# The mixers' gate and branch products with tokens as stationary columns, 512 weight columns moving, and a transpose of the gated sum on TensorE

## The chip, the cores and the metric

The kernel runs on one core of one Trainium2 chip. The metric is the device time of one execution in microseconds (us). TensorE (PE in the profile) multiplies, VectorE (DVE) and ScalarE (ACT) copy, split and combine, GpSimd (POOL) does a few small powers, SyncE (SP) starts the transfers from HBM. A matmul of TensorE holds a 128x128 stationary operand, loaded by a weight load (PEld), and streams a moving operand of up to 512 columns past it into one of eight PSUM banks.

## The reference

Float32 throughout, 256 tokens, width 1024. Two layers of a first block, each with a mixer between two feed-forward parts, then two more mixers with their feed-forwards. The change is in the mixers of the first block, of which there are two:

```python
h = rms_norm(x, mix_norm[l])
(c_q, c_kv, k_rope, g_q, g_k, g_v, g_b, g_a, g_z, m_qkv, gate_logits) = split_cols(h @ w_in[l], IN_SPLITS)
o_mla, o_gdn, o_moba = ...                                # three branches, 512 wide each
branches = jnp.stack([o_mla, o_gdn, o_moba], axis=2)
up = jnp.einsum('bsnw,nwd->bsnd', branches, w_branch[l])  # 3 x (512 -> 1024)
gates = jax.nn.sigmoid(gate_logits.reshape(b, s, N_BRANCH, D_MODEL))
x = x + jnp.sum(gates * up, axis=2) @ w_out[l]
```

## The kernel before

All weights stream from HBM in units of 128x1024 floats (512 KB). A unit goes through four hands. SP loads it into one of three `raw` slots (L501). ACT rounds it to a first part `w_hi` (`split` on ACT, L558). DVE subtracts that from `raw` and so makes the rest, `w_lo` (L1229). TensorE uses the two parts in three products, high by high, high by low and low by high, with the activations `a_hi` and `a_lo`. There are six slots for split units, and the splits run five units ahead (`AHEAD`): ACT's `split(u + AHEAD)` waits until unit u-1 has been used. Every engine runs its own list of instructions in a fixed order that is written out by hand, with semaphores between the lists.

In a mixer, 24 gate units and 12 branch units are spread among the other work as fillers: TensorE runs them while other engines do the steps of the recurrence (`cover`), of the two softmax attentions (`FILLS`, four rounds each: fill, scores of the next pair, turn of P, fill, product with V) and of the projections between them. Gate units 0 to 3 stand in `cover`, 4 to 8 between the steps after it, 9 to 17 in the first attention, 18 to 21 after it, and the second attention has 22, 23 and branch units 0 to 7. Branch units 8 to 11 follow, and then the eight units of `w_out`.

One gate unit (`gate_unit`, by `fm`) makes 128 gate features of 256 tokens. Its stationary operand is a 128x128 block of weights and its moving operand is 256 tokens: 8 blocks of the contraction by 3 products, 24 matmuls of 256 columns into half a bank. ACT makes the tanh of it (`gate_tile`, L685, 128x256) and counts `gate_evac`. Units alternate between banks 6 and 7, so each waits for the tanh of the one before the last. One branch unit (`branch_unit`) makes 256 features of one branch in the same way, 24 matmuls of 256 columns into a whole bank, and DVE's `merge` multiplies it by (1 + tanh) into `mB` (L1465, counts `merge_read`) and adds that to `msum` (L1469). `msum` has features on partitions and tokens along, as the product with `w_out` wants its stationary operand, so ACT and DVE split it into `a_hi` (L910) and `a_lo` (L1826) straight from SBUF.

The lines that the next sections use, beside those: L694 and L696 are the exponentials of `exp_scores`, with their sums (ACT); L1434 to L1442 are `score_max`, which ends in `nmax_ready` (DVE); L1450 to L1452 are `normalise`; L1456 is `o_low`; L897 copies the turned keys (ACT); L1811 ends the keys of the second attention (DVE); L2168 is the helper of all matmuls; L2679, L2619 and L2452 are transposes.

## Time and profile before

| | before |
|---|---|
| time, median of 3 runs | 1932.98 us (1932.57 to 1933.21) |
| the profiled execution | 1932.31 us |
| its span in the trace | 1930.5 us |
| TensorE busy | 1922.0 us, 13137 matmuls |
| DVE, ACT, POOL busy | 1470.1, 1088.4, 85.6 us |
| DMA queue 1, share of 16 engines | 52.0% |

The span is the time from the first to the last instruction of the program; about 1.8 us of the execution lie around it. Matmuls overlap in the records (the end of each is modelled), so what a matmul costs is read from the distance between two starts, not from its own length. "Idle before" in the groups is the time in which an engine stood before an instruction, with the engine and line that released it.

### The profile page before, as it was taken

What the parts mean: (1) busy time and instruction counts of PE and PEld (TensorE: products, weight loads), DVE (VectorE), ACT (ScalarE), POOL (GpSimd) and SP (SyncE); (2) the same over time, 40 slices, a digit from 0 to 9 for tenths busy, and PEclk for the clock granted to TensorE, in tenths of its full rate; (3) what the DMA queues carried; (4) which work ended last, traced back from release to release, by engine and by line L of the source; (5) the groups of instructions that cost most, each with busy time, mean ns of one, the idle gap of its engine ahead of it and who ended that gap; (6) DMA issues with size and microseconds to landing.
All of it is one profiled execution on the core that took longest, in us unless ns stands there. A gap on an engine that the chain in (4) does not pass through costs nothing.

```text
span 1930.5 us, 35082 instructions
## 1 busy us (share of the span) xinstructions
PE 1922.0 (100%) x13137; PEld 1729.2 (90%) x13137; DVE 1470.1 (76%) x2252; ACT 1088.4 (56%) x1702; POOL 85.6 (4%) x61
## 2 busy tenths in 40 slices
PE   9999999999999999999999999999999999999999
PEld 8888999999888888889899998889898889889998
DVE  6777887777777777778777777777577888887887
ACT  6555764664555555567546644555355656676554
POOL 0000012010000000000110102000000000110000
PEclk9999999999999999999999999999999999999999
DMA  6656552344555555555424455655655555544654
GB/s 232 199 188 201 165 175 89 121 153 155 163 194 187 194 175 193 187 186 183 135 98 145 142 159 174 196 189 190 205 176 170 196 189 175 164 141 155 194 186 142
DMA packets 95798, 331.03 MB, mean 171 GB/s; under 512 B 10960, under 2 KB 16720, under 8 KB 95568
## 3 DMA queue, kind: packets, MB, share of 16 engines
q1 hardware_dynamic: 93712, 325.91, 52.0%
q10 hardware_dynamic: 1984, 3.68, 0.5%
q8 instruction: 74, 1.21, 0.3%
q14 instruction: 28, 0.23, 0.0%
HBM read 327.91 MB, written 1.64 MB: 171 GB/s over the span
## 4 chain that ended last, share of the span: by engine, by line
PE 93%; issue 3%; DVE 2%; ACT 1%; DMA 1%; POOL 0%; POOLq 0%; DVEq 0%; SPq 0%; ACTq 0%
PE ps L2168 91%; DMA raw<-stream 1%; DVE w_lo L1229 1%; PE ps L2194 1%; PE ps L2452 1%; PE ps L2679 0%; ACT w_hi L558 0%; DVE a_both L1286 0%; POOL sc L1144 0%; PE ps L2619 0%; DVE tmp L1254 0%; DVE a_both L1344 0%; DVE arena L1339 0%; ACT arena L783 0%; DVE sc L2032 0%
## 5 line engine op out<-in xcount | busy, mean ns | idle before, releaser
L2168 PE MATMUL ps<-a_both,w_hi 128*128 128x256 f32 (+1 forms) x4864 | 994.4, 325 | 0.4
L1229 DVE TENSOR_TENSOR w_lo<-raw,w_hi 128x1024 fp32r<-128x1024 f32 x614 | 749.9, 1227 | 236.3 <-ACT w_hi L558 235.5
L2168 PEld LDWEIGHTS ps<-a_both,w_hi 128*128 128x128 f32 x4864 | 813.4, 190 | 78.3 <-issue 3.2
L558 ACT ACTIVATE w_hi<-raw 128x1024 fp32r<-128x1024 f32 x614 | 637.1, 1053 | 139.5 <-DMA raw<-stream 91.6
L2168 PE MATMUL ps<-a_both,w_lo 128*128 128x256 f32 x3344 | 660.5, 283 | 0.0
L2168 PEld LDWEIGHTS ps<-a_both,w_lo 128*128 128x128 f32 x3344 | 524.4, 191 | 8.9
L2168 PE MATMUL ps<-w_hi,a_both 128*128 128x512 f32 (+2 forms) x1616 | 506.0, 383 | 0.3
L2168 PEld LDWEIGHTS ps<-w_hi,a_both 128*128 128x128 f32 x1616 | 300.8, 188 | 56.8 <-DVE a_both L1344 0.8
L2168 PE MATMUL ps<-w_lo,a_both 128*128 128x512 f32 (+2 forms) x808 | 308.6, 382 | 0.0
L2168 PEld LDWEIGHTS ps<-w_lo,a_both 128*128 128x128 f32 x808 | 152.4, 189 | 24.1
L629 ACT ACTIVATE a_both<-arena 128x256 fp32r<-128x256 f32 x132 | 55.3, 419 | 144.2 <-DVE arena L1339 101.1
L1144 POOL TENSOR_TENSOR sc<-sc,nhalf 128x2 f32<-128x2 f32 (+5 forms) x25 | 58.7, 2349 | 1620.8 <-DVE sc L1268 1185.9
L618 ACT ACTIVATE arena<-arena 128x256 f32<-128x256 f32 x88 | 36.7, 417 | 159.6 <-DVE arena L1331 143.9
L1298 DVE TENSOR_TENSOR arena<-ps,arena 128x512 f32<-128x512 f32 x114 | 78.6, 690 | 39.1 <-ACT arena L623 37.7
L623 ACT ACTIVATE arena<-ps 128x512 f32<-128x512 f32 x114 | 67.9, 596 | 65.9 <-PE ps L2168 65.8
L1331 DVE TENSOR_TENSOR arena<-arena 128x512 f32<-128x512 f32 x114 | 77.9, 684 | 0.0
L919 ACT ACTIVATE arena<-arena,par 128x256 f32<-128x256 f32 x44 | 26.5, 601 | 88.2 <-DVE arena L1331 78.4
L1344 DVE TENSOR_TENSOR a_both<-arena,a_both 128x256 fp32r<-128x256 f32 x132 | 56.4, 427 | 7.2 <-ACT a_both L629 7.2
L1837 DVE SCALAR_TENSOR_TENSOR arena<-arena,par 128x255 f32<-128x255 f32 x44 | 21.3, 484 | 37.6 <-ACT arena L919 37.5
L685 ACT ACTIVATE gates<-ps 128x256 f32<-128x256 f32 x48 | 18.5, 385 | 46.7 <-PE ps L2168 46.4
L2168 PE MATMUL ps<-arena 128*128 128x128 f32 (+4 forms) x400 | 43.8, 321 | 0.4 <-ACT gates L811 0.4
L1339 DVE SCALAR_TENSOR_TENSOR arena<-arena 128x256 f32<-128x256 f32 x88 | 39.0, 443 | 3.0
(334 smaller groups left out, 1238.5 us busy)
## 6 DMA issues: line engine op xcount, KB each, us to landing
raw<-stream SPq DMA_DIRECT2D x613, 512.0 KB, 3.4
arena<-upad SPq DMA_DIRECT2D x8, 284.0 KB, 5.4
gates<-late ACTq DMA_DIRECT2D x1, 1088.0 KB, 5.7
out<-tmp SPq DMA_DIRECT2D x8, 128.0 KB, 2.0
upad<-arena ACTq DMA_DIRECT2D x2, 288.0 KB, 7.7
con<-consts SPq DMA_DIRECT2D x1, 560.0 KB, 5.2
raw<-stream ACTq DMA_DIRECT2D x1, 512.0 KB, 4.3
x<-x_in SPq DMA_DIRECT2D x2, 256.0 KB, 5.4
```

Source lines behind the costliest of these rows:

```text
L558: nc.scalar.activation(w_hi[:, u % SLOTS, :], raw[:, u % RAW, :], ACT.Copy).then_inc(hi_ready, 1)
L618: nc.scalar.activation(th2[:, p, :], gus[:, p, 0:TOK], ACT.Tanh, scale=0.5).then_inc(gate_act, 1)
L623: nc.scalar.activation(glo, ps[:, 4 + 2 * p:6 + 2 * p, TOK:512], ACT.Copy).then_inc(lo_copied, 1)
L629: nc.scalar.activation(a_hi[:, 8 + p, :], gu2[:, p, :], ACT.Copy).then_inc(gu_hi_ready, 1)
L919: nc.scalar.activation(gh2[:, p, :], gus[:, p, 0:TOK], ACT.Identity, scale=w, bias=b).then_inc(conv_in, 1)
L1144: return nc.gpsimd.tensor_tensor(o, i, nhalf[:, 0:n], ALU.pow)
L1229: V.tensor_tensor(w_lo[:, u % SLOTS, :], raw[:, u % RAW, :], w_hi[:, u % SLOTS, :], ALU.subtract).then_inc(split_ready, 1)
L1298: V.tensor_tensor(gus[:, p, :].rearrange("p (a b) -> p a b", b=TOK), ps[:, 4 + 2 * p:6 + 2 * p, 0:TOK], glo, ALU.add).then_inc(gu_added, 1)
L1331: V.tensor_tensor(v, v, each(rrow, 2), ALU.mult).then_inc(gs_ready, 1)
L1339: V.scalar_tensor_tensor(gu2[:, p, :], a2[:, p, :], 0.25, gus[:, p, TOK:512], ALU.mult, ALU.mult).then_inc(gu_ready, 1)
L1344: V.tensor_tensor(a_lo[:, 8 + p, :], gu2[:, p, :], a_hi[:, 8 + p, :], ALU.subtract).then_inc(gu_split, 1)
L2168: return nc.tensor.matmul(o, a, b, start=start, stop=stop, **k)
```

## The change

Three things in the two mixers are written anew.

The operands of gates and branches change places. Each matmul now holds 128 tokens and streams 512 weight columns. The slots are loaded by another pattern (`RELAID`): a gate unit is two blocks of the contraction by 512 features, put together from four stretches of 256 columns (1 KB) per partition, and four such units make one group g of 512 features; a branch unit is two blocks by 512 features, from two stretches of 512 columns (2 KB), and two make a group. `token_half` is half a unit: 128 tokens, 6 matmuls of 512 columns into bank 6 (first 128 tokens) or bank 7 (the others). A unit is 12 matmuls. A group's sum stays in the two banks over all its units, so `gate_evac`, `merge_read` and the waits on them come once per group and token half, not once per unit.

ACT makes a tanh of 128x512 twice per group, for the first half at `gate_half` and for the second when the group's last unit is used; for three of four units `gate_tile` does nothing. DVE multiplies and adds in two parts of 128x512 for each branch group (`merge_factor`, `merge_add`). `msum` now has tokens on partitions, so TensorE turns it (`mix_turn`, 8 transposes for each half of the features) into banks 4 to 7, and the split for `w_out` reads those banks.

The order moves with it: two branch units (`branch_early`) go before the `up` units, gates 16 and 17 behind them, and the product order at the end is branch 8 to 10, the first half of 11, the first turn, the rest of 11, `w_out` 0 and 1, the second turn, `w_out` 2 to 7.

```diff
+        branch = group(("branch", l), 12)
+        take(("branch_early", l), branch[:2])
-        for n, name in ((1, "branch_gdn"), (2, "branch_moba"), (0, "branch_mla")):
-            take((name, l), [AT["branch", l] + 3 * dp + n for dp in range(4)])
+        take(("branch", l), branch[2:])
...
-EARLY_GATES = 18
+EARLY_GATES = 16
+BRANCH_OF = (1, 1, 2, 2, 0, 0)
+def gate_at(l, i):
+    return POS["gates", l] + i if i < EARLY_GATES else POS["late_gates", l] + i - EARLY_GATES
+def branch_at(l, i):
+    return POS["branch_early", l] + i if i < 2 else POS["branch", l] + i - 2
+def relaid():
+    at = {}
+    for l in range(DEPTH):
+        for i in range(24):
+            at[gate_at(l, i)] = (AT["gates_" + "abc"[i // 8], l] + i % 8 // 4 * 4, 1, 4, 256 * (i % 4))
+        for i in range(12):
+            g = i // 2
+            at[branch_at(l, i)] = (AT["branch", l] + 6 * (g % 2) + BRANCH_OF[g], 3, 2, 512 * (i % 2))
+    return at
+RELAID = relaid()
...
-         ((("g", 15),), (("g", 16),)))
-FILLS = (FILLS, (((("g", 22), ("g", 23)), (("b", 0),)),) + tuple(((("b", 2 * j - 1),), (("b", 2 * j),)) for j in range(1, 4)))
-LAST_FILL = (("g", 17), ("b", 7))
+         ((("g", 15),), (("b", 0),)))
+FILLS = (FILLS, (((("g", 20), ("g", 21)), (("g", 22),)),
+                 ((("g", 23),), (("b", 2),)),
+                 ((("b", 3),), (("b", 4),)),
+                 ((("b", 5),), (("b", 6),))))
+LAST_FILL = (("b", 1), ("b", 7))
...
+                elif u in RELAID:
+                    lo, step, n, col = RELAID[u]
+                    src = stream[lo:lo + step * n].rearrange("(i s) p n -> p i s n", s=step)
+                    sp.dma_start(raw[:, u % RAW, :].rearrange("p (i n) -> p i n", i=n), src[:, :, 0, col:col + UC // n]
+                                 ).then_inc(raw_loaded[u % RAW], 16)
...
+                if i % 4 < 3:
+                    return
+                act.wait_ge(gate_half, 6 * l + i // 4 + 1)
+                nc.scalar.activation(gate_part(i // 4, 0), bank(6), ACT.Tanh, scale=0.5).then_inc(gate_evac, 1)
-                nc.scalar.activation(gates[:, i, :], bank(6 + i % 2, 0, TOK), ACT.Tanh, scale=0.5).then_inc(gate_evac, 1)
+                nc.scalar.activation(gate_part(i // 4, 1), bank(7), ACT.Tanh, scale=0.5).then_inc(gate_evac, 1)
...
-                for dp in range(4):
-                    split(POS["branch_mla", l] + dp + AHEAD)
-                    if dp:
-                        mix_high(l, dp - 1)
+                for i in range(8, 12):
+                    split(branch_at(l, i) + AHEAD)
+                mix_high(l, 0)
+                mix_high(l, 1)
+                split(POS["out", l] + AHEAD)
+                split(POS["out", l] + 1 + AHEAD)
+                mix_high(l, 2)
-                for k in range(KC):
+                for k in range(2, KC):
-                act.wait_ge(mix_ready, 4 * l + dp + 1)
-                nc.scalar.activation(a_hi[:, 2 * dp:2 * dp + 2, :], msum[:, dp, :].rearrange("p (a b) -> p a b", b=TOK), ACT.Copy).then_inc(mix_hi, 1)
+                act.wait_ge(mix_turned, 4 * l + dp + 1)
+                nc.scalar.activation(a_hi[:, 2 * dp:2 * dp + 2, :], bank(4 + dp).rearrange("p (a b) -> p a b", b=TOK), ACT.Copy).then_inc(mix_hi, 1)
...
+            added_at = {}
+            def merge_factor(l, g):
+                n, h = BRANCH_OF[g], g % 2
+                if 2 < g < 5:
+                    need(added_at[g - 1])
+                elif g == 5:
+                    dve.wait_ge(mix_ready, 4 * l + 2)
+                for tt in range(TT):
+                    if tt == 0:
+                        dve.wait_ge(branch_half, 6 * l + g + 1)
+                        dve.wait_ge(unit_used, branch_at(l, 2 * g + 1) + 1)
+                    V.scalar_tensor_tensor(mB[:, tt, :] if g > 1 else msum[:, 2 * h + tt, :], gate_part(2 * n + h, tt), 1.0, bank(6 + tt),
+                                           ALU.add, ALU.mult).then_inc(merge_read, 1)
+            def merge_add(l, g):
+                h = g % 2
+                if g > 1:
+                    for tt in range(TT):
+                        dve.wait_ge(merge_read, 12 * l + 2 * g + tt + 1)
+                        a = V.tensor_tensor(msum[:, 2 * h + tt, :], msum[:, 2 * h + tt, :], mB[:, tt, :], ALU.add)
+                        if g < 4:
+                            added_at[g] = tick(a)
+                        else:
+                            a.then_inc(mix_ready, 1)
+            def merge(l, g):
+                merge_factor(l, g)
+                merge_add(l, g)
...
+                    if kind and j > 1:
+                        merge_factor(l, j - 1)
...
-                    if kind and j:
-                        merge(l, 2 * j - 1)
+                    if kind and j > 1:
+                        merge_add(l, j - 1)
-                    if kind:
-                        merge(l, 2 * j)
-                if kind:
-                    merge(l, 7)
+                merge(l, 3 if kind else 0)
...
-                    split(POS["branch_mla", l] + dp + AHEAD)
-                    merge(l, 8 + dp)
+                def mix_low(dp):
+                    V.tensor_tensor(a_lo[:, 2 * dp:2 * dp + 2, :], bank(4 + dp).rearrange("p (a b) -> p a b", b=TOK), a_hi[:, 2 * dp:2 * dp + 2, :],
+                split(branch_at(l, 8) + AHEAD)
+                merge(l, 4)
+                for i in range(9, 12):
+                    split(branch_at(l, i) + AHEAD)
+                mix_low(0)
+                mix_low(1)
+                merge(l, 5)
+                split(POS["out", l] + AHEAD)
+                split(POS["out", l] + 1 + AHEAD)
+                mix_low(2)
+                mix_low(3)
+                for k in range(2, KC - 1):
...
+            def token_half(u, b, chunk, n, first, last, tt):
+                s, tk = u % SLOTS, slice(128 * tt, 128 * tt + 128)
+                wh, wl = (w[:, s, :].rearrange("p (i k n) -> p i k n", i=n, k=2) for w in (w_hi, w_lo))
+                o = bank(b).rearrange("p (i n) -> p i n", i=n)
+                for k in range(2):
+                    mm(o, a_hi[:, chunk + k, tk], wh[:, :, k, :], start=(first and k == 0), stop=False)
+                    mm(o, a_hi[:, chunk + k, tk], wl[:, :, k, :], start=False, stop=False)
+                    i = mm(o, a_lo[:, chunk + k, tk], wh[:, :, k, :], start=False, stop=(last and k == 1))
+                return i
+            def gate_unit(l, i, tts=range(TT)):
+                g, q, u = i // 4, i % 4, gate_at(l, i)
+                for tt in tts:
+                    if q == 0:
+                        if g == 0:
+                            pe.wait_ge(zs_ready, 2 * l + tt + 1)
+                        elif g != 4:
+                            pe.wait_ge(gate_evac, 12 * l + 2 * (g - 1) + tt + 1)
+                        elif tt == 0:
+                            pe.wait_ge(merge_read, 12 * l + 1)
+                        else:
+                            pe.wait_ge(*AC.at(l, "qcopy"))
+                    if tt == 0:
+                        pe.wait_ge(split_ready, u + 1)
+                    e = token_half(u, 6 + tt, 2 * q, 4, q == 0, q == 3, tt)
+                    if tt == 0 and q == 3:
+                        e.then_inc(gate_half, 1)
+                if TT - 1 in tts:
+                    e.then_inc(unit_used, 1)
+            def branch_unit(l, i, between=None):
+                g, q, u = i // 2, i % 2, branch_at(l, i)
+                for tt in range(TT):
+                    if q == 0:
+                        if g < 2:
+                            pe.wait_ge(gate_evac, 12 * l + (8 if g == 0 else 12) - 1 + tt)
+                        else:
+                            pe.wait_ge(merge_read, 12 * l + 2 * (g - 1) + tt + 1)
+                    if tt == 0:
+                        pe.wait_ge(split_ready, u + 1)
+                    e = token_half(u, 6 + tt, 8 + 4 * BRANCH_OF[g] + 2 * q, 2, q == 0, q == 1, tt)
+                    if tt == 0 and q == 1:
+                        e.then_inc(branch_half, 1)
+                    if tt == 0 and between is not None:
+                        between()
+                e.then_inc(unit_used, 1)
+                if f == ("b", 0):
+                    pe.wait_ge(*DV.at(l, "oz_lo"))
...
-                pe.wait_ge(gate_evac, 24 * l + EARLY_GATES)
+                pe.wait_ge(merge_read, 12 * l + 2)
...
-                for dp in range(4):
-                    branch_unit(l, 8 + dp)
+                def mix_turn(h):
+                    pe.wait_ge(mix_ready, 4 * l + 2 * h + 2)
+                    for c in range(4):
+                        for tt in range(TT):
+                            i = nc.tensor.transpose(bank(4 + 2 * h + c // 2, (c % 2) * TOK + 128 * tt, (c % 2) * TOK + 128 * tt + 128),
+                                                    msum[:, 2 * h + tt, 128 * c:128 * c + 128], ident)
+                        if c % 2:
+                            i.then_inc(mix_turned, 1)
+                for i in range(8, 11):
+                    branch_unit(l, i)
+                branch_unit(l, 11, lambda: mix_turn(0))
+                    if k == 2:
+                        mix_turn(1)
```

On ACT, between the first and the second attention, this stood before, from the turned queries to the first two fills:

```order
L895 ACTIVATE arena<-ps 96x1024 [waits pe_step] x2
L897 ACTIVATE tmp<-ps,sc 96x1024 [waits pe_step]
L558 ACTIVATE w_hi<-raw 128x1024 [waits unit_used,raw_loaded0]
L685 ACTIVATE gates<-ps 128x256 [waits unit_used]
L558 ACTIVATE w_hi<-raw 128x1024 [waits unit_used,raw_loaded1]
L694 ACTIVATE arena,sc<-ps,sc 128x128 [waits nmax_ready]
L696 ACTIVATE arena,sc<-ps,sc 128x256
L694 ACTIVATE arena,sc<-ps,sc 128x128
L696 ACTIVATE arena,sc<-ps,sc 128x256
L685 ACTIVATE gates<-ps 128x256 [waits unit_used]
L897 ACTIVATE tmp<-ps,sc 96x1024 [waits pe_step]
```

And this stands there now (L594 is `split`, L734 and L736 are the exponentials, L723 and L725 the two tanhs of group 4):

```order
L935 ACTIVATE arena<-ps 96x1024 [waits pe_step] x2
L937 ACTIVATE tmp<-ps,sc 96x1024 [waits pe_step]
L594 ACTIVATE w_hi<-raw 128x1024 [waits unit_used,raw_loaded0]
L594 ACTIVATE w_hi<-raw 128x1024 [waits unit_used,raw_loaded1]
L734 ACTIVATE arena,sc<-ps,sc 128x128 [waits nmax_ready]
L736 ACTIVATE arena,sc<-ps,sc 128x256
L734 ACTIVATE arena,sc<-ps,sc 128x128
L736 ACTIVATE arena,sc<-ps,sc 128x256
L723 ACTIVATE gates<-ps 128x512 [waits gate_half]
L725 ACTIVATE gates<-ps 128x512 [waits unit_used]
L937 ACTIVATE tmp<-ps,sc 96x1024 [waits pe_step]
```

The tanh between the two splits is gone, and both of group 4 stand behind the four exponentials, where one of two 128x256 tanhs stood.

On PE, at the same place, the turned keys are followed by the first fill of the second attention. Before (`L2679` the transposes; `gate_evac` is the tanh of the unit before the last):

```order
L2679 MATMUL ps<-con,arena 96x128 x8
L2168 MATMUL ps<-a_both,w_hi 128x256 [waits split_ready,gate_evac]
L2168 MATMUL ps<-a_both,w_hi 128x256
L2168 MATMUL ps<-a_both,w_lo 128x256
L2168 MATMUL ps<-a_both,w_hi 128x256 x2
```

Now (`L2774` the transposes, unit 20 is the first of group 5 and waits for the tanh of group 4, whose last unit is the one just ahead of the transposes):

```order
L2774 MATMUL ps<-con,arena 96x128 x8
L2236 MATMUL ps<-w_hi,a_both 128x512 [waits split_ready,gate_evac]
L2236 MATMUL ps<-w_lo,a_both 128x512
L2236 MATMUL ps<-w_hi,a_both 128x512 x2
L2236 MATMUL ps<-w_lo,a_both 128x512
L2236 MATMUL ps<-w_hi,a_both 128x512
L2236 MATMUL ps<-w_hi,a_both 128x512 [waits gate_evac]
```

The wait has the same name at the same place, but it now stands for the tanh of the group that has just ended.

At the end of a mixer PE has now, from the last matmul of branch unit 11's first half to the first unit of `w_out`:

```order
L2236 MATMUL ps<-w_hi,a_both 128x512
L2796 MATMUL ps<-con,arena 128x128 [waits mix_ready]
L2796 MATMUL ps<-con,arena 128x128 x7
L2236 MATMUL ps<-w_hi,a_both 128x512
L2236 MATMUL ps<-w_lo,a_both 128x512
L2236 MATMUL ps<-w_hi,a_both 128x512 x2
L2236 MATMUL ps<-w_lo,a_both 128x512
L2236 MATMUL ps<-w_hi,a_both 128x512
L2236 MATMUL ps<-w_hi,a_both 128x512 [waits split_ready,mix_split]
```

The eight transposes (L2796) are new, and half a branch unit stands between them and the unit that needs what they turned.

## Rows read from the trace of the kernel before

**Rows 1.** The page: busy us, share of the span, instructions; granted clock in 40 slices

```profile
PE 1922.0 (100%) x13137; PEld 1729.2 (90%) x13137; DVE 1470.1 (76%) x2252; ACT 1088.4 (56%) x1702; POOL 85.6 (4%) x61
...
PEclk9999999999999999999999999999999999999999
...
PE 93%; issue 3%; DVE 2%; ACT 1%; DMA 1%; POOL 0%; POOLq 0%; DVEq 0%; SPq 0%; ACTq 0%
```

**Rows 2.** Weight loads' waits in layer 0's mixer: waiting, released by, total us, times, longest

```profile
PEld ps L2168 <- DVE arena L1465: 0.8, 3, 0.3
...
PEld ps L2679 <- DVE arena L1811: 0.2, 1, 0.2
```

**Rows 3.** Stretches of equal matmuls: length, then busy us and instructions of each engine, clock

```profile
1652.01:1684.44 32.43, 32.43 (x144) 26.85 (x143) 26.89 (x40) 26.01 (x39) 4.49 (x1) 1.00 0.58 184
451.25:465.52 14.27, 14.27 (x120) 14.27 (x120) 12.74 (x18) 6.51 (x8) 0.00 (x0) 1.00 0.44 148
```

**Rows 4.** Timeline: eight transposes, then a fill; start us, us, engine, line, operation

```profile
413.59 1.03 PE L2679 MATMUL ps<-con,arena 128*96 128x128 f32 x8
414.38 0.48 PE L2168 MATMUL ps<-a_both,w_hi 128*128 128x256 f32 x2
```

**Rows 5.** Timeline: eight short matmuls among 512-column ones

```profile
268.69 0.94 PE L2168 MATMUL ps<-ones,tmp 128*128 128x1 f32 x8
...
269.49 0.49 PE L2168 MATMUL ps<-w_hi,a_both 128*128 128x512 f32 x1
...
269.82 0.40 PE L2168 MATMUL ps<-w_lo,a_both 128*128 128x512 f32 x1
```

**Rows 6.** Timeline at the place of rows 4: DVE and ACT

```profile
409.61 0.38 ACT L685 ACTIVATE gates<-ps 128x256 f32<-128x256 f32 x1 [0.80 <-PE ps L2168]
409.89 1.05 ACT L558 ACTIVATE w_hi<-raw 128x1024 fp32r<-128x1024 f32 x1
410.98 1.23 DVE L1229 TENSOR_TENSOR w_lo<-raw,w_hi 128x1024 fp32r<-128x1024 f32 x1 [0.90 <-ACT w_hi L558]
...
414.11 0.16 DVE L1442 SCALAR_TENSOR_TENSOR sc<-sc 128x4 f32<-128x4 f32 x1
414.31 0.46 ACT L694 ACTIVATE arena<-ps,sc 128x128 f32<-128x128 f32 x1 [3.37 <-DVE sc L1442]
...
416.28 0.39 ACT L685 ACTIVATE gates<-ps 128x256 f32<-128x256 f32 x1
```

**Rows 7.** Timeline in `cover`: ACT's copies of U, and the matmuls that wait for them

```profile
301.01 1.20 ACT L823 ACTIVATE gates<-ps 64x512 f32<-64x512 f32 x2 [0.60 <-PE ps L2168]
...
302.52 0.68 PE L2168 MATMUL ps<-gates,arena 64*64 64x64 f32 x16
```

**Rows 8.** DVE's groups in layer 0's mixer: count, busy us, mean ns, idle before

```profile
L1229 DVE TENSOR_TENSOR w_lo<-raw,w_hi 128x1024 fp32r<-128x1024 f32 x48 | 59.6, 1245 | 17.3 <-ACT w_hi L558 17.1
L1465 DVE SCALAR_TENSOR_TENSOR arena<-gates,ps 128x512 f32<-128x512 f32 x12 | 8.2, 679 | 0.0
...
L1469 DVE TENSOR_TENSOR arena<-arena 128x512 f32<-128x512 f32 x8 | 5.5, 692 | 0.3
```

**Rows 9.** Timeline: from the last scores of the second attention to the last turn

```profile
439.01 0.82 PE L2452 MATMUL ps<-con,arena 128*128 128x128 f32 x6
...
444.28 0.68 DVE L1452 TENSOR_TENSOR arena<-arena,sc 128x512 f32<-128x512 f32 x1
...
446.50 0.82 PE L2452 MATMUL ps<-con,arena 128*128 128x128 f32 x6
```

**Rows 10.** Timeline: ACT's and DVE's split behind the last pair of the second attention

```profile
451.31 1.05 ACT L558 ACTIVATE w_hi<-raw 128x1024 fp32r<-128x1024 f32 x1
...
453.27 0.42 DVE L1456 TENSOR_TENSOR a_both<-ps,a_both 128x256 fp32r<-128x256 f32 x1
...
453.60 1.22 DVE L1229 TENSOR_TENSOR w_lo<-raw,w_hi 128x1024 fp32r<-128x1024 f32 x1
```

**Rows 11.** SP's loads, us to landing: the four of L498 (1 KB stretches)

```profile
DMA to landing us min/median/max: 3.4/4.2/5.4
```

**Rows 12.** The same for the 283 loads of L501 (4 KB stretches)

```profile
DMA to landing us min/median/max: 3.0/3.4/9.6
```

51 lines of the change are left out of this document (7 added, 44 removed).

## The prediction

> **What bounds the kernel now.** I read the page first. [...] So the kernel takes what its 13137 matmuls take, plus the few moments in which PE waits. In a mixer these are short: over layer 0's mixer its weight loads waited some 0.8 us for DVE's merge and 0.2 us for its keys [rows 2]. So there are only two questions: what a matmul costs in the new form, and which waits of PE the new order makes. Work that DVE or ACT saves is worth nothing unless PE waits for it.
>
> The price of a matmul is read from long stretches of one form. A stretch of 512-column matmuls has 32.43 us for 143 starts, 0.2268 us each; the last units of a mixer, 256 columns each, have 14.27 us for 119 starts, 0.1199 us each [rows 3] (the profile counts one more, which had started before the stretch). Two of 256 cost 0.2398 us and one of 512 costs 0.2268 us, for the same product. A matmul costs some 0.013 us on top of its columns in either form, and the change pays that half as often.
>
> **The matmuls.** A unit goes from 24 x 0.1199 = 2.878 us to 12 x 0.2268 = 2.722 us, 0.156 us less. There are 36 units in each of two mixers: 72 x 0.156 = **11.2 us less**. The moving operand is new in one thing: it lies in two or four stretches instead of one row of 512. No matmul of the trace streams such an operand. The nearest row is the 512-column stretch, which I take. The bound above is that it streams no better than two matmuls of 256, 0.2398 us, and nothing is gained; below, that it costs the same as now.
>
> [...]
>
> **The transposes.** Added are two `mix_turn` of 8 transposes in each mixer. Eight transposes took 0.79 us from their first start to the next matmul [rows 4]. Eight short matmuls between ones of 512 columns took 0.80 us and the first one behind them 0.33 instead of 0.23 us [rows 5]. That is 0.90 us a time, four times: **3.6 us more**. All of it is on the path, since PE has no free time. Both rows say the same of the eight, so I give it no more room than 3.2 us (without the pause at the change of form) to 3.9.
>
> **Waits that go.** The list has three waits for DVE's merge in a mixer, 0.8 us together [rows 2]. A weight load pauses at each change of form anyway, wait or not, so I count only 0.1 us of each as a wait that can go. A group waits only once for its bank now, and the merge is done by then: 2 x 3 x 0.1 = **0.6 us less**.
>
> **The tanh of group 4.** This is the place that decides. Unit 20, the first fill of the second attention, begins group 5 in bank 6, and must wait until ACT has taken the tanh of group 4 from there. Group 4 ends with unit 19, the last thing that PE does ahead of it but for eight transposes. On ACT that tanh stands behind the four exponentials of the first pair, and these wait for DVE's maximum. Before, this was harmless: the fill in its place waited for the unit before the last, long done.
>
> PE now comes to it at 413.59 + 0.79 = 414.38 us on the scale of the old trace [rows 4]. Between the wait for the keys (next paragraph) and here lie units 18 and 19, so it will be there 2 x 0.15 us earlier, at 414.1. ACT began its exponentials at 414.31, 0.04 us behind the end of DVE's L1442, and was through at 416.28 [rows 6]. How much earlier can they be? The chain ahead was: tanh 409.61 (gone now), `split` 409.89 to 410.94, DVE's split 410.98 to 412.21, the scaling L1819, the maximum. Without the tanh, ACT's split can start where the tanh did, 0.28 us earlier, and unit 18 is used 0.14 us earlier, so the whole chain is some 0.4 us earlier. So the exponentials end at about 415.9. A tanh of 512 columns takes 0.6 us (two copies of that length took 1.20 us, [rows 7]). PE starts unit 20 at 416.5, after a wait of 416.5 - 414.1 = 2.4 us. Two mixers: **4.8 us more**. Bounds: 2.0 us if the chain is earlier than I work out, 3.0 us if it is not earlier at all, so 4 to 6 us for both.
>
> Behind the waiting fill PE has units 20 and 21 and then the scores of the second pair, so everything of the second attention moves back by that much. DVE and ACT get time by it, but nobody else waits for PE who could give something back.
>
> **The keys.** PE already waits for DVE's L1811 at the third set of transposes [rows 2]. Gates 16 and 17 ahead of it are 0.31 us shorter together, and DVE's chain is not: it hangs on the products of the `up` units and a power on POOL. So this wait grows by 0.3 us: **0.6 us more** for two mixers, and the gain of two units is lost there.
>
> **Banks at the end of the second attention.** The merge of group g must have read bank 6 before group g + 1 starts. DVE makes it, with a first multiplication of 0.68 us, behind a split of some 1.2 us [rows 8]. For branch unit 6, I count from the end of the last pair's scores, at 439.01 in the old trace. DVE had normalised that pair at 444.96, 5.95 us behind it [rows 9]; with that split and multiplication it is through 7.8 us behind it. PE began the last turn 7.49 us behind the same point [rows 9]; two fills shorter and a wait gone make 7.1, and with a turn of some 0.6 us PE is there after 7.7 us: a wait of 0.2 us, with the signal. For branch unit 8: DVE's last o_low ended at 453.69 and its split at 454.82, because the split on ACT ended at 452.36 only [rows 10]. With the adds of the group before ahead of o_low, as now, o_low ends at 452.6, the split at 453.8 and the multiplication at 454.5; PE is there when the last fill ends: the old one ran 24 matmuls on from about 451.1, to 454.0, the new one is done by 453.8, and less its own wait of 0.2 us at unit 6 it would be earlier still. A wait of some 0.7 us. Then the first `w_out` unit waits up to 0.1 us for its split. In sum 0.9 us for each mixer, **1.8 us more**, with bounds of 0.4 and 5 us: both are differences between two long chains, and an error of 0.3 us in a link goes into them in full.
>
> **What costs nothing.** In `cover`, half a unit is now 0.08 us shorter, and the next matmuls wait for ACT's copies. These ended at 302.21 and the matmuls started at 302.52 [rows 7]; 0.3 us of cover less 0.08 leaves 0.2. ACT's tanhs of group 0 come once at the end of it. The loads of gate units have stretches of 1 KB. The four loads of that kind took 3.4 to 5.4 us with a median of 4.2 [rows 11], against 3.4 us for the others [rows 12]. In the mixer a load is issued three splits ahead of its use, 8 us or more at ACT's pace there (48 splits in the 195 us of a mixer, [rows 8], are 4 us each), so even 5.4 us are hidden; without that cover, a load that lands 1 us late would cost 1 us at most once per unit. DVE's multiplications and adds are as many and as long as before (12 and 8, [rows 8]).
>
> **The sum.** -11.2 + 3.6 - 0.6 + 4.8 + 0.6 + 1.8 = -1.0 us. The profiled execution took 1932.31 us, so it would take 1931.3; the median of the runs is 0.7 us above that execution, so the forecast is **1932.0 us**. A measurement of this kernel can tell about 0.2% (3.9 us) from no change, and this is well inside it.
>
> **The rivals.**
> First, the wait at group 4 is not there, because the exponentials or PE's arrival lie otherwise than I read them. Then 4.8 us of the sum fall away: 1927.2 us, faster. For it speaks only that both times come from one execution; against it, that the order of ACT is fixed and the tanh stands behind the exponentials in it.
> Second, on the other side: the chains at the end of the second attention are longer than I count. The mechanism is DVE's: its multiplication for branch groups 2 and 3 stands behind a split that waits for ACT's exponentials or o_high, and then each of the waits at branch units 6 and 8 is 1.5 us longer. Two places in two mixers at 1.5 us are 6 us: 1938.0 us, slower. It decides from 0.7 us more at each of these waits on. For it speaks that DVE is the fullest engine after PE; against it, that DVE still idled 17.3 us for ACT's splits in this mixer [rows 8].
> Third, a moving operand in four stretches streams slower than a row, at the upper bound above: then nothing of the 11.2 us comes, and the time is 1932.0 + 11.2 = 1943.2 us, slower. Nothing in the trace shows it either way. [...]
> Fourth, that the change does not do what it says: the sum would then be that of the old form with the new waits, which is the third rival's.
>
> **Chances.** Forecast 0.62 (1930 to 1935 us); first rival 0.17; second 0.13; third with the page's gap 0.08. Faster by over 0.2% (under 1929.1) has the first, 0.17; within 0.2%, 0.62; slower by over 0.2% (over 1936.8), 0.21. The range takes in the first rival and the second, and leaves the third and the tails out: 1926.5 to 1938.5 us.
>
> **What would show it.** In the profile of the changed kernel: 864 matmuls more of 512 columns and 1728 fewer of 256, and a stretch of branch units at 0.227 us each (if 0.24, the third rival). PE waiting 2.4 us behind the eight transposes before the second attention, released by ACT's tanh (if under 1 us, the first). Waits of 0.2 and 0.7 us for the merge's multiplication (over 1 us, the second). Two turns of 0.8 us in each mixer. A wait of 0.4 us in place of 0.14 for the keys. The forecast would be wrong if loads became late, which ACT's splits would show as waits for the DMA inside the mixers, or if one of the small sums on which PE's arrivals rest is off, as each wait is a small difference.

## The result, and the profile after

| | before | changed |
|---|---|---|
| time, median of 8 runs each | 1932.93 us (1932.15 to 1933.80) | 1938.71 us (1937.00 to 1945.28) |
| ratio to before | | 1.0034, 95% interval 1.0025 to 1.0042 |
| span of the profiled execution | 1930.5 us | 1936.2 us |

The changed kernel is slower by 0.34%, 5.8 us. The forecast was 1932.0 us, no change that can be measured, with a range up to 1938.5 us: the time lies just outside.

One correction to the diff above: in `merge_factor` an `else:` stands between the wait for `branch_half` and the one for `unit_used`. The first half's multiplication waits for the first half of the unit alone, the second half's for the whole unit.

From the page of the changed kernel, the lines that answer to [rows 1], with the sum of TensorE's matmuls and the queue q8:

```profile
PE 1919.0 (99%) x12305; PEld 1681.9 (87%) x12305; DVE 1470.3 (76%) x2252; ACT 1086.2 (56%) x1678; POOL 84.8 (4%) x61
...
q8 instruction: 67, 1.10, 0.2%
...
PE 90%; issue 3%; DVE 3%; DMA 2%; ACT 1%; POOL 0%; SPq 0%; POOLq 0%; DVEq 0%; ACTq 0%
```

There are 832 matmuls fewer: 864 saved, and 32 transposes more. PE is busy 3 us less than before and the span is 5.7 us longer, so most of the loss is in waits. (Matmuls at the lower clock count as busy; that part comes below.) The chain shows where to look: PE's share fell from 93% to 90%, and DMA's rose from 1% to 2%.

The waits of PE's weight loads over the whole changed kernel (who waits, for whom, total us, times, longest):

```profile
PEld ps L2236 <- ACT gates L723: 4.9, 2, 2.5
...
PEld ps L2914 <- DVE arena L2114: 1.9, 1, 1.9
...
PEld ps L2774 <- DVE arena L1869: 1.0, 2, 0.5
```

The first row is the wait for the tanh of group 4, twice 2.4 to 2.5 us, as forecast. The third is the keys' wait, 0.5 instead of 0.2 us a time. The second is not in a mixer that was changed: it stands at 1693 us, in a mixer of the second block, whose code is the same as before. There PE waited 0.4 us and now waits 1.9.

The timeline of PE at the first of the two long waits (start us, us, engine, line, operation, idle before):

```profile
410.93 1.04 PE L2774 MATMUL ps<-con,arena 128*96 128x128 f32 x8
414.17 0.54 PE L2236 MATMUL ps<-w_hi,a_both 128*128 128x512 f32 x1 [2.21 <-ACT gates L723]
414.50 0.63 PE L2236 MATMUL ps<-w_lo,a_both 128*128 128x512 f32 x1
414.93 1.05 PE L2236 MATMUL ps<-w_hi,a_both 128*128 128x512 f32 x2
415.79 0.63 PE L2236 MATMUL ps<-w_lo,a_both 128*128 128x512 f32 x1
416.21 1.05 PE L2236 MATMUL ps<-w_hi,a_both 128*128 128x512 f32 x2
```

And on ACT the reason: the last exponential, then the two tanhs that PE waits for:

```profile
411.55 0.46 ACT L734 ACTIVATE arena<-ps,sc 128x128 f32<-128x128 f32 x1 [3.36 <-DVE sc L1485]
...
413.51 0.60 ACT L723 ACTIVATE gates<-ps 128x512 f32<-128x512 f32 x1
413.99 0.61 ACT L725 ACTIVATE gates<-ps 128x512 f32<-128x512 f32 x1
```

Behind the wait stands something that the forecast did not have: from 414.50 us on, three matmuls take 1.29 us (414.50 to 415.79), 0.43 us each where a long stretch has 0.227. The stretches of the same kernel around both waits (length, busy us and instructions of PE, PEld, DVE, ACT, POOL, granted clock, DMA share, GB/s):

```profile
411.00:414.17 3.17, 0.96 (x9) 0.71 (x8) 0.95 (x4) 2.62 (x10) 0.00 (x0) 1.00 0.56 191
414.50:417.90 3.40, 3.40 (x9) 2.64 (x8) 1.63 (x2) 2.03 (x3) 0.00 (x0) 0.50 0.00 0
...
1077.50:1080.60 3.10, 0.95 (x9) 0.70 (x7) 0.88 (x4) 2.58 (x10) 0.00 (x0) 1.00 0.54 195
1080.98:1086.22 5.24, 5.24 (x25) 4.32 (x23) 2.85 (x3) 3.09 (x4) 0.00 (x0) 1.00 0.13 43
```

In layer 0 (first two rows) the granted clock is 0.50 for 3.4 us behind the wait, which is 1.7 us of work lost. Behind the wait of the same length in layer 1 (last two rows) it stays at 1.00. The forty slices of the profile's page show nothing of it, since a 9 is 90% or more. In layer 0 PE had been busy for 0.96 of 3.17 us before the clock fell; in layer 1 it had been busy for 0.95 of 3.10 us and the clock stayed, so this figure alone does not decide it here.

### The profile page after: what moved, and what is told of

Same layout as the page of the kernel before. It is cut to its first block, busy times and chain, and to the rows that moved or that the text cites. A ratio compares the mean times of both kernels' runs of the same rounds, so it can differ in the third digit from the quotient of the medians.

```text
span 1936.2 us, 33344 instructions
## 1 busy us (share of the span) xinstructions
PE 1919.0 (99%) x12305; PEld 1681.9 (87%) x12305; DVE 1470.3 (76%) x2252; ACT 1086.2 (56%) x1678; POOL 84.8 (4%) x61
## 4 chain that ended last, share of the span: by engine, by line
PE 90%; issue 3%; DVE 3%; DMA 2%; ACT 1%; POOL 0%; SPq 0%; POOLq 0%; DVEq 0%; ACTq 0%
PE ps L2236 88%; DMA raw<-stream 1%; DVE w_lo L1272 1%; ACT w_hi L594 1%; PE ps L2262 1%; PE ps L2547 1%; DMA arena<-upad 0%; DVE a_both L1329 0%; POOL sc L1187 0%; PE ps L2714 0%; PE ps L2796 0%; DVE tmp L1297 0%; DVE tmp L2110 0%; DVE arena L1868 0%; PE ps L2774 0%
## 5 line engine op out<-in xcount | busy, mean ns | idle before, releaser
L2236 PE MATMUL ps<-a_both,w_hi 128*128 128x512 f32 (+1 forms) x3712 | 778.2, 337 | 0.7 <-DVE a_both L1329 0.7
L594 ACT ACTIVATE w_hi<-raw 128x1024 fp32r<-128x1024 f32 x614 | 637.5, 1053 | 166.9 <-DMA raw<-stream 92.5
L2236 PE MATMUL ps<-w_hi,a_both 128*128 128x512 f32 (+2 forms) x2192 | 704.6, 389 | 5.4 <-ACT gates L723 4.4
L2236 PEld LDWEIGHTS ps<-a_both,w_hi 128*128 128x128 f32 x3712 | 634.8, 190 | 73.7 <-DVE w_lo L1272 1.5
L2236 PE MATMUL ps<-a_both,w_lo 128*128 128x256 f32 x2768 | 497.9, 283 | 0.0
L2236 PEld LDWEIGHTS ps<-w_hi,a_both 128*128 128x128 f32 x2192 | 409.6, 189 | 89.9 <-ACT gates L723 4.9
L2236 PE MATMUL ps<-w_lo,a_both 128*128 128x512 f32 (+2 forms) x1096 | 422.3, 385 | 0.0
L2236 PEld LDWEIGHTS ps<-a_both,w_lo 128*128 128x128 f32 x2768 | 414.3, 191 | 8.9
L2236 PEld LDWEIGHTS ps<-w_lo,a_both 128*128 128x128 f32 x1096 | 206.9, 189 | 33.3
L2236 PEld LDWEIGHTS ps<-arena 128*64 128x64 f32 (+2 forms) x400 | 31.7, 166 | 13.7 <-issue 8.5
```

What stands on the lines that cost most here:

```text
L594: nc.scalar.activation(w_hi[:, u % SLOTS, :], raw[:, u % RAW, :], ACT.Copy).then_inc(hi_ready, 1)
L2236: return nc.tensor.matmul(o, a, b, start=start, stop=stop, **k)
```

## The experiments

All times are medians; the kernel before, run beside them on the same chips, had 1932.6 to 1932.95 us. The mean clock is the granted clock over one whole execution, to three digits. One stretch of 3.4 us at half clock takes 0.0009 off it, and 1.7 us of work.

### The changed kernel again, and two ways at the long wait

c1_changed_again is the changed kernel, unedited.

> The changed kernel as it is, a second profile of it. In its first profile the two waits for group 4's tanh took 2.4 us each, ten matmuls behind the one in layer 0 took 0.43 us instead of 0.227 (2.0 us, granted clock 0.55 there), and four waits outside the mixers were 2.9 us longer than before. If these belong to the kernel, they are here again at the same places; if the lower clock and the waits outside come and go from run to run, at least one of them is elsewhere or absent, with a time between 1936 and 1940 us.

Measured: 1939.37 us (1936.16 to 1942.82, 8 runs), ratio 1.0031 (1.0020 to 1.0042). The waits of 2.4 us were there in both mixers. The clock fell behind both of them, and a third time behind a wait of 2.5 us at 1695 us. The second and third of these falls:

```profile
1081.50:1084.90 3.40, 3.40 (x9) 2.62 (x9) 1.73 (x2) 2.13 (x3) 0.00 (x0) 0.50 0.03 5
1695.90:1699.30 3.40, 3.40 (x18) 3.40 (x17) 3.37 (x5) 1.54 (x1) 1.07 (x1) 0.50 0.46 154
```

So the long waits belong to the kernel, and the fall of the clock comes and goes behind them. In both profiles of the changed kernel the waits outside the changed mixers are longer than before.

e1_tanh_first:

```diff
                         exp_scores(8 * l + 4, None, sc[:, 192:208])
-                        late_gate(3)
...
+                        late_gate(3)
                         exp_scores(8 * l + 4, None, sc[:, 192:208])
```

> The two tanhs of gate group 4 stand on ACT ahead of the four exponentials of the second attention's first pair, nothing else is moved. Theory (the wait and the clock behind it): the waits of 2.4 us in each mixer go, and with them the slow matmuls in layer 0, so 4.9 + 2.0 = 6.9 us less than the changed kernel, 1931.8 us, within 0.1% of the kernel before. Rival (the wait alone costs, the low clock comes from elsewhere): 4.9 us less, 1933.8 us, with ten matmuls at 0.43 us still in the trace. Second rival (the gain is given back at the next wait, DVE's exponent chain): under 2 us less, with a wait of 1 us or more at the first turn of P.

Measured: 1932.63 us (1929.93 to 1934.70, 11 runs), 6.7 us less than the changed kernel beside it. The waits for L723 are gone, and its profile has no half-clock stretch in the mixers. The theory gave 6.9 us less. Nothing is given back at the next wait. 4.7 to 4.9 us of it are the two waits, so some 1.8 us are left for the clock, about one fall per execution. Against the first median of the changed kernel (1938.71 us) it would be some 1.3 us; e7 and e8 below measure a single fall more directly.

e2_wait_filled makes the last eight transposes of the keys four times:

```diff
-                    for h in range(h0, h0 + 4):
+                    for h in (tuple(range(h0, h0 + 4)) * (4 if name == "kT1" else 1)):
```

> The changed kernel with the eight transposes of the second half of the turned keys made four times over (24 more, 2.6 us of PE work), so that PE works through the time in which it waited for group 4's tanh. They do the same work again, so the data is the same. Theory (the idle time lowers the clock): unit 20 starts 0 to 0.3 us later than in the changed kernel, since its tanh comes when it did, but no matmul behind it takes 0.43 us: 2.0 us less in layer 0 of the profiled run, less 0.5 us for the work beyond the wait, so 0 to 2 us less than the changed kernel by the median. Rival (the low clock has another cause, the activity of the whole stretch): ten matmuls of 0.43 us are there again, and the time is 0.2 to 0.6 us longer.

Measured: 1940.45 us (1936.27 to 1941.54, 5 runs), not less than the changed kernel. In its profile:

```profile
926.00:932.70 6.70, 6.61 (x45) 5.63 (x44) 6.70 (x14) 4.71 (x4) 0.00 (x0) 1.00 0.50 163
932.70:939.50 6.80, 6.80 (x22) 5.64 (x21) 1.81 (x2) 4.46 (x10) 0.00 (x0) 0.50 0.72 228
410.90:414.10 3.20, 3.20 (x30) 3.10 (x29) 0.98 (x4) 2.40 (x9) 0.00 (x0) 1.00 0.57 198
414.20:417.90 3.70, 3.70 (x20) 3.11 (x19) 1.89 (x3) 2.93 (x5) 0.00 (x0) 1.00 0.02 4
```

With the wait filled, the clock stays at 1.00 at 414 us, as the theory says. But it was at 0.50 for 6.8 us from 932.7 us on, where no long wait precedes: PE was busy for 6.61 of the 6.70 us before, with 16 matmuls of one column among others. In four of the five executions the mean clock was 0.998, no higher than in the changed kernel. The forecast of a gain is a miss, and e2 does not show that the idle time lowers the clock. That the fall at 414 us went by the filling is one execution's evidence; why another came at 932.7 us stays open. The edit also has a second effect: it adds 96 instructions to TensorE's list, and the runs further down show that such a shift can move the time by itself.

### One wait alone, in the kernel before

e7_wait_alone lets the first fill of the second attention, and no other unit, wait for the tanh of the unit just ahead:

```diff
-                    pe.wait_ge(gate_evac, 24 * l + i - 1)
+                    pe.wait_ge(gate_evac, 24 * l + i - (i != 22))
```

> The kernel before with one thing of the change alone: the first fill of the second attention (gate 22) waits for the tanh of the unit just ahead (gate 21), which stands behind the four exponentials on ACT, not for the one before that. Theory (wait and clock): PE waits 2.4 us there in both mixers, and in most executions the clock falls to 0.5 for 3.4 us behind one or both waits, which costs 1.7 us each: 4.8 us more by the waits and 0 to 3.4 by the clock, 1937.8 to 1941.1 us, median near 1940. Rival (only the waits cost): 1937.7 us, with the spread of the kernel before. Second rival (the time is given back later by shorter waits): under 1936 us.

Measured: 1937.59 us (1936.98 to 1939.13, 10 runs), 4.8 us over the kernel before, ratio 1.0027 (1.0017 to 1.0036). The waits of its weight loads over the whole span:

```profile
PEld ps L2168 <- ACT gates L685: 5.4, 4, 2.4
```

and the stretches of the wait and behind it in layer 0:

```profile
414.40:416.90 2.50, 0.48 (x4) 0.48 (x5) 0.74 (x3) 2.50 (x10) 0.00 (x0) 1.00 0.32 131
416.90:420.30 3.40, 3.40 (x31) 3.40 (x30) 1.69 (x2) 2.11 (x4) 0.00 (x0) 1.00 0.02 5
```

The price of the wait is its own length, 2 x 2.4 us, and none of it comes back later: the second rival is out. The clock stayed at 1.00 behind this wait. The ten executions fall into two groups: six with a mean clock of 1.000 (1937.0 to 1937.7 us) and four with 0.999 (1938.6 to 1939.1 us). So in this kernel a fall is an extra of some 1.5 us in less than half of the executions, and the median shows the waits only: between theory and first rival, nearer to the rival. A mean clock of 0.999 is a weak sign by itself: three of the 28 executions of the kernel before show it (1931.8 to 1932.7 us) and are not slower, and the profile of e1 has it with no half-clock stretch but one at the end of the program (mean clock 0.77 over the last 4.8 us). Here it is the gap in the times that goes with it.

### The loads, and the waits outside the mixers

e3_loads_alone is the kernel before with the table `RELAID` and the lines for SP's loads that use it (as in the diff above), and nothing else.

> The kernel before with the changed kernel's loads alone: its gate units come in stretches of 1 KB and its branch units of 2 KB. The gates and branches are multiplied with other blocks of the weights than they should be, so the output is not the reference's; every instruction is that of the kernel before. Theory (the loads cost nothing): 1933.0 us, within 0.5 us of the kernel before, and the waits outside the mixers as before. Rival (the loads cost, by landing later or by what they do to the transfers behind them): 2 to 3 us more, 1935 to 1936 us, with waits of PE or ACT for DMA at the mixers or behind them.

Measured: 1932.83 us (1932.37 to 1933.92, 11 runs), ratio 1.0000 (0.9991 to 1.0009). Stretches of 1 and 2 KB cost nothing that this can measure, as forecast, inside the mixers or behind them. What lengthens the waits outside is something else.

In the changed kernel's unchanged stage at 1693 us, DVE is late since ACT's split is late, and that is late since the loads are. SP's loads ahead of it (four of each kernel, us to landing), the changed kernel first, then the kernel before:

```profile
DMA to landing us min/median/max: 3.3/4.6/4.8
```

```profile
DMA to landing us min/median/max: 3.3/3.9/4.2
```

With the tanhs first (e1) the loads are later still, and ACT's split waits 3.2 us for one of them (timeline, then SP's three loads there):

```profile
1673.83 1.06 ACT L594 ACTIVATE w_hi<-raw 128x1024 fp32r<-128x1024 f32 x1 [3.18 <-DMA raw<-stream]
```

```profile
DMA to landing us min/median/max: 4.4/5.2/5.4
```

In e1 the DMA queues in that stretch (packets, MB, share of 16 engines) hold one more thing than the loads:

```profile
q8 instruction: 1, 0.02, 0.7%
```

The page calls q8's kind "instruction". Its packets are of 16 KB, and there are 74 of them before (1.21 MB) and 67 after (1.10 MB): seven fewer, for 1720 instructions of TensorE fewer (832 matmuls, each with its weight load, and 56 waits), which is 246 a packet. They go with TensorE's list: in the kernel before, it starts 192 to 325 instructions between two neighbouring packets (matmuls, weight loads and waits; 67 distances, mean 255.7), whether DVE starts 3 in that time or 44 and ACT 4 or 51; in the changed kernel the mean of 60 is 255.6. So the runs below take a packet for 256 instructions of TensorE, and for its code, as the author reads these counts. Six more gaps of the kernel before have 1535 to 1899 instructions, six times as many and more, so the trace seems not to hold every packet. A packet falls among these loads in e1_tanh_first (1671 us) and in both profiles of the changed kernel (1675 and 1679 us); the kernel before has its packets at 1652 and 1682 us, and none between. Counted back from the end of TensorE's list, the packet of 1682 us comes 3469 instructions ahead of it, those of the changed kernel 3562 and 3550, and that of e1 3552. The next two kernels test whether that is the cause. Waits that are met already are put between the 512-column matmuls of `w_out`; they do nothing. Of each group of them all but one become instructions of their own: the traces hold 72 and 184 instructions more. In e5 the edit is:

```diff
+            def more(n=[0]):
+                n[0] += 1
+                m = EXTRA * n[0] // 96 - EXTRA * (n[0] - 1) // 96
+                for _ in range(m + 1 if m else 0):
+                    pe.wait_ge(consts_set, 1)
...
+                        if extra:
+                            more()
                         mm(o, a_hi[:, chunk, tk], w_hi[:, s, w], start=first, stop=False)
```

e5_before_shifted (72 of them, in layer 0):

> The kernel before, and 72 waits that are met already on PE in the w_out of layer 0's mixer, nothing else: 1720 + 72 = 7 x 256, so TensorE's code is fetched at the phase that it has in the changed kernel. Theory (code packets beside the loads): a packet comes at about 1673 us, two or three weight loads from 1670 us on take 5 us instead of 3.3 to 4.2, the wait at the second block's first DVE wait (362 ns over the step before) is about 2 us: 1935 us, 2 us over the kernel before. Rival (chance, or the new order itself): 1933 us, as the kernel before.

Measured: 1935.73 us (1934.37 to 1938.17, 11 runs), 2.9 us over the kernel before, ratio 1.0014 (1.0005 to 1.0023). PE's wait at that stage, the landing of the loads there, and q8 in the same stretch:

```profile
PEld ps L2820 <- DVE arena L2047: 1.8, 1, 1.8
```

```profile
DMA to landing us min/median/max: 3.4/4.5/4.8
```

```profile
q8 instruction: 1, 0.02, 1.2%
```

The packet comes at 1673.9 us, 3562 instructions ahead of the end of TensorE's list, as in the first profile of the changed kernel.

e4_first_and_shifted (the tanhs first, and 184 met waits in both mixers):

> The kernel with the two tanhs first, and with 184 waits more on PE that are met already (96 in the w_out of each mixer less 8), each an instruction of its own between matmuls of 512 columns. They bring TensorE's code, which is fetched in packets of 256 instructions (16 KB), back to the phase that it has in the kernel before, whose list is 1720 instructions longer (1720 - 184 = 6 x 256). Theory (in the new kernels a packet of code goes through the DMA engines at 1671 to 1679 us, beside three weight loads that then land 1 to 2 us late, and the mixers of the second block wait 2 us): the packets come at 1652 and 1682 us as in the kernel before, the wait of 2.2 us at the first of those transposes is 0.4 us, and the time is 2 us less than with the tanhs first alone: 1930.6 us, 0.12% less than the kernel before. Rival (the late loads are chance): 1932.6 us as without them, or more if the waits cost.

Measured: 1929.46 us (1928.69 to 1929.88, 11 runs), 3.2 us less than with the tanhs first alone, ratio to before 0.9982 (0.9973 to 0.9991). The answering rows; the stretch has no row of q8, whose packet comes at 1678.0 us, behind these loads and 3475 instructions ahead of the end of the list (3469 in the kernel before):

```profile
PEld ps L2927 <- DVE arena L2115: 0.5, 1, 0.5
```

```profile
DMA to landing us min/median/max: 3.3/4.2/4.4
```

Both ways the time follows the position of the code: an edit that computes nothing makes the kernel before 2.9 us slower, and the new order 3.2 us faster. That extra waits would cost time by themselves is out, since 184 of them go with a gain. The clock is no part of it in these profiles: e1, e4 and e5 have no half-clock stretch between the first 10 us and the last 6. All eleven profiles of this document agree on the stage at 1690 us. Where a packet of q8 falls among the loads (the changed kernel twice, e1, e5), PE waits 1.8 to 2.5 us there; where none does (the kernel before, e2, e3, e4, e6, e7, e8), 0.4 to 0.6 us. That is 1.4 of e5's 2.9 us and 1.7 of e4's 3.2. The rest, and with it what goes beyond the 2 us expected, arises elsewhere: in the profile of e5 the distance to the kernel before also grows by 0.5 us at 896 us and by 0.8 at 929 us. Whether packets cause that part as well was not traced. In e4 the spread of the runs is small too, 1.2 us, against 4.8 us with the tanhs first alone.

e8_code_shift_alone (the changed kernel with the 184 met waits, the tanhs where they were):

> The changed kernel with the 184 met waits alone: the tanhs of group 4 stay behind the exponentials. Theory (three separate costs that add up: the two waits of 2.4 us, the clock behind them, the phase of the code): 3.2 us less than the changed kernel, as the same waits gave with the tanhs first, so about 1936.0 us, and no late loads at 1670 to 1680 us; the waits of 2.4 us stay, and the granted clock falls behind them in some executions, by 1.7 us each time. Rival (the code's phase and the clock act together, so that one alone explains both): below 1935 us, at the level of waits alone, with no fall of the clock in any execution, or above 1938 us.

Measured: 1936.40 us (1934.24 to 1937.90, 11 runs), ratio 1.0019 (1.0010 to 1.0029): 2.3 to 3.0 us less than the two medians of the changed kernel. The costs add up, nearly. In its profile (mean clock 0.998) the clock fell behind both long waits. With the code's position out of the way, the eleven executions separate by the mean clock: one with 1.000 took 1934.2 us, four with 0.999 took 1935.7 to 1936.1, and six with 0.998 took 1936.4 to 1937.9. That fits no fall, one fall and two, at some 1.6 us each. The one without a fall lies 4.8 us above e4, which is the price of the two waits alone.

### A version that beats both

e6_dve_earlier is e4 with two moves on DVE:

```diff
                 o_low(n0 + 3, chunk + 3)
+                if kind:
+                    merge_factor(l, 3)
                 split(fill_at(l, LAST_FILL[kind]) + AHEAD)
-                merge(l, 3 if kind else 0)
+                if kind:
+                    merge_add(l, 3)
+                else:
+                    merge(l, 0)
...
-                split(gc + AHEAD)
                 dve.wait_ge(*PO.at(l, "mlarsk"))
...
+                split(gc + AHEAD)
                 link(V.tensor_reduce(ssq, qsq.rearrange("p (a b) -> p a b", b=LD), AX.X, ALU.add))
```

> The kernel of the run with the tanhs first and the code shifted, with two moves on DVE: the multiplication of branch group 3 stands ahead of the split behind the last o_low, and the split of gate 16 stands behind the keys, not ahead of them. Theory (both waits of PE hang on DVE's order): the wait of 0.43 us at branch unit 8 and that of 0.4 us at the second block of turned keys go, in both mixers, 1.7 us less: 1929 us, 0.2% less than the kernel before. Rival (the later splits make a load or a unit late): a new wait for w_lo in the mixers, no gain, 1930.5 us or more.

Measured: 1927.48 us (1927.13 to 1927.86, 7 runs), 0.9971 of the kernel before (0.9960 to 0.9983). That is 5.3 us faster than before and 11 us faster than the changed kernel. Against e4 it is 2.0 us, where 1.7 were expected. Both waits are gone. DVE multiplies the first half before the unit is done:

```profile
448.69 0.69 DVE L1517 SCALAR_TENSOR_TENSOR arena<-gates,ps 128x512 f32<-128x512 f32 x1 [0.32 <-PE ps L2242]
450.01 0.69 DVE L1517 SCALAR_TENSOR_TENSOR arena<-gates,ps 128x512 f32<-128x512 f32 x1 [0.63 <-PE ps L2242]
```

## Why the prediction was wrong

The forecast was 0.9 us less than before, measured are 5.8 us more. Two steps failed. The term for the matmuls was too large, 11.2 us where 8.0 came. And two costs were put at nothing without a reason: the clock behind a long wait, and the unchanged code. The paragraphs below go through the terms.

**The wait at group 4: right.** 2.4 us in each mixer was forecast; 2.37 and 2.36 were measured, as the distance of the starts less the 0.11 us that a transpose takes in a row of them. Both its causes were right, ACT's order and PE's early arrival; e1 and e7 show it from both sides. The first rival, with no wait there, is out.

**The clock behind it: missing.** The forecast let a wait cost its own length. It costs some 1.6 us more whenever the clock falls behind it (e8): once in the first profile, in the second behind both of them and a third time elsewhere. By e1 that is some 1.8 us of the median. What brings a fall on, no run shows.

**The matmuls: the term that was mis-sized.** The price was right: 40 starts in the branch units at the end of the mixer had 9.08 us (two more records touch the stretch's edges), 0.227 us each as in [rows 3], and the third rival (0.24 us) is out. There the moving operand lies in two stretches. With four, as in the gate units, the distance of the starts was 0.227 us too, in the last ten of the 24 matmuls of a long fill (three fills, median). So neither form cost more here than the row of 512 columns.

```profile
455.16:464.24 9.08, 9.08 (x42) 7.46 (x41) 6.88 (x9) 3.45 (x4) 0.00 (x0) 1.00 0.32 113
```

Wrong was to take that price for units which stand alone among other work. One fill between a turn of P and its product, before and after (timelines; the first rows show where the stretch begins, the last what follows it):

```profile
447.08 0.48 PE L2168 MATMUL ps<-a_both,w_hi 128*128 128x256 f32 x2
447.39 0.28 PE L2168 MATMUL ps<-a_both,w_lo 128*128 128x256 f32 x1
...
450.11 0.44 PE L2168 MATMUL ps<-arena 128*64 128x256 f32 x2
```

```profile
447.50 0.48 PE L2236 MATMUL ps<-w_hi,a_both 128*128 128x512 f32 x1
447.82 0.40 PE L2236 MATMUL ps<-w_lo,a_both 128*128 128x512 f32 x1
...
450.41 0.44 PE L2236 MATMUL ps<-arena 128*64 128x256 f32 x2
```

Before, 3.03 us (447.08 to 450.11); after, 2.91 (447.50 to 450.41): 0.12 us less, not 0.156. Other fills saved 0.07 to 0.14 us, half a unit in `cover` 0.04 instead of 0.08. By the starts in the two traces, the 33 changed stretches up to the last fill saved 3.25 us in a mixer, where 31 units at 0.156 make 4.8, and the five units behind them the full 0.8. So the term is -8.0 us in place of -11.2 us. The difference lies where a stretch begins and ends: over its matmuls' long-stretch price the fill above had 0.15 us before (3.03 - 2.88) and has 0.19 now (2.91 - 2.72), and a mean of 0.05 us is lost in each of the 33 stretches. In the changed kernel a stretch of gate units that ran at the full clock had 0.31 to 0.34 us between its first two starts in 49 of 53 cases (median 0.335), and 0.23 from then on.

**The transposes: right.** The turns took 0.79 us and 0.09 at the next matmul, 0.88 for the 0.90 forecast. The forecast put such a pause at each change of form. The trace of the kernel before has it behind transposes (0.32 us for two starts of 256 columns at the median of 65 places, where a stretch has 0.24), and not where 256 columns follow 512 (0.233 at the median of 107 places).

```profile
464.24 1.03 PE L2796 MATMUL ps<-con,arena 128*128 128x128 f32 x8
465.03 0.47 PE L2236 MATMUL ps<-w_hi,a_both 128*128 128x512 f32 x1
465.34 0.40 PE L2236 MATMUL ps<-w_lo,a_both 128*128 128x512 f32 x1
```

**Keys and banks.** The keys' wait grew by 0.25 us a mixer (0.3 forecast). At branch unit 6 there was no wait (0.2 forecast), at unit 8 one of 0.43 us (0.7). So the banks cost 0.9 us for both mixers, not 1.8. The trace names no releaser for that wait; that it is for DVE's multiplication follows from e6, where it went when that multiplication was moved ahead. The second rival, longer chains at this place, gave nearly the right time (1938.0) for a wrong reason.

**The rest of the program: missing.** "Unchanged code takes what it took" was assumed without a word. With 1720 instructions of TensorE fewer, the packets of q8 meet the weight loads at other moments (a packet at 1675 and 1679 us, where the kernel before has none between 1652 and 1682), and the position of the list is worth 3.2 us (e4 against e1; 2.9 us the other way round in e5). Late loads were named as a sign of being wrong, but inside the mixers, and no term was given to them; they came outside.

The sum by these (matmuls, turns, merge waits gone at the forecast's 0.6, group 4, keys, banks): -8.0 + 3.5 - 0.6 + 4.7 + 0.5 + 0.9 = +1.0 us in the mixers, and 1.8 us for the clock and 3.2 for the code's position make 6.0; measured are 5.8 and, in the second comparison, 6.4 us. e4 has neither the wait at group 4 nor the moved packets, and so tests the other terms by themselves: -8.0 + 3.5 - 0.6 + 0.5 + 0.9 = -3.7 us, and measured are -3.4 (1929.46 against 1932.82 us). Of the miss of 6.7 us, then, about 2 are in the terms of the sum and 5 in two mechanisms that it had no term for.

## What to carry to other kernels

Price a matmul by its place: the gain of a wider moving operand is read off stretches as short as the ones that will run, with the step at their beginning (here 0.12 us for a fill, where long stretches promised 0.156). A wait of PE like the 2.4 us here cost its length and sometimes a slow stretch behind it (some 1.6 us), so an engine's order is looked at for a result that PE needs at once and that stands behind work it doesn't need, as the tanh behind the exponentials. When a change takes away or adds hundreds of instructions, compare the same kernel with some instructions that do nothing: if the time moves by microseconds, part of the verdict is the position of the code and not the idea.

## What was not expected of the hardware

Packets of 16 KB that the page calls "instruction" go with TensorE's list while the kernel runs: 67 to 74 of them, at a mean distance of 255 to 257 of its instructions in each of the eleven profiles (the six longer gaps left out). The page counts them against the same 16 engines as the loads of weights, and a packet took one engine's time of 0.9 to 1.8 us among the loads shown here (0.7 to 1.4% of 16 engines over 8 us). Where one fell among back-to-back loads of 512 KB, these landed later: at the stage shown, the median went from 3.9 us in the kernel before to 4.6 in the changed one, and from 4.2 to 5.2 with the tanhs first (e4 and e1). There ACT's split waited 3.2 us for a load (e1), and PE 1.8 to 2.5 us instead of 0.4 to 0.6. The position of the code as a whole was worth 3 us of 1930 (3.2 in e4, 2.9 in e5), with no instruction of the computation changed. The clock fell to 0.50 for 3.4 us behind an idle time of 2.4 us, and not always: by mean clock and time it fell at least once in 4 of 10 executions of e7 and in 10 of 11 of e8, and in the profile of e2 it fell, for 6.8 us, without such an idle time at all. What decides it, the runs do not show.
